# Storing the S5 inputs of a decoder trunk apart by tap instead of in token order

## The reference

```python
def s5_mix(u, ...):                                   # u: (1, 528, 256), 16 groups of 16 channels
    ...                                               # lam, bb from a, log_dt, b
    bu_re = jnp.einsum('gnc,blgc->blgn', bb_re, ug)
    bu_im = jnp.einsum('gnc,blgc->blgn', bb_im, ug)
    _, _, h_re, h_im = lax.associative_scan(complex_linear_combine, (lam_re, lam_im, bu_re, bu_im), axis=1)
    y = (jnp.einsum('gcn,blgn->blgc', c_re, h_re)
         - jnp.einsum('gcn,blgn->blgc', c_im, h_im)).reshape(bsz, length, S5_DIM)
    y = jax.nn.gelu(y + d_skip * uf)
    return y * jax.nn.sigmoid(y @ glu_w + glu_b)
```

## Time and profile before

| | us |
|---|---|
| median of three runs | 1577.77 (1576.98 to 1577.96) |
| the profiled execution | 1578.03 |
| its span, first to last instruction | 1576.3 |
| TensorE busy | 1533.4 (97%) |
| VectorE busy | 873.2 (55%) |
| ScalarE busy | 696.6 (44%) |
| passes that read UIN by tap: scan inputs, 128 | 7.8 |
| passes that read UIN by tap: kernel taps, 40 | 11.3 |

### The profile page before, as it was taken

One profiled execution on the slowest core, in us unless ns is written; L12 is line 12 of the kernel. 1 busy time (PEld: TensorE's weight loads), 2 busy tenths in 40 slices (PEclk: granted clock), 3 DMA queues, 4 the chain that ended last, 5 costly groups with the idle time before them and its releaser, 6 DMA issues.

```text
span 1576.3 us, 38948 instructions
## 1 busy us (share of the span) xinstructions
PE 1533.4 (97%) x16258; PEld 1443.3 (92%) x16258; DVE 873.2 (55%) x1487; ACT 696.6 (44%) x1120; POOL 118.4 (8%) x257
## 2 busy tenths in 40 slices
PE   8999999999999999999999999999899999999998
PEld 7899898999699999999999999965599999999886
DVE  5578744443556667666333445366556666765222
ACT  5555233333535444444222588367635444443121
POOL 1450293300000000000000000000000000000000
PEclk9999999999999999999999999999999999999999
DMA  5222000000123333233323232330023333324331
GB/s 155 68 67 81 21 4 4 4 4 4 44 68 93 93 93 87 86 93 95 99 85 86 65 92 80 84 122 1 1 81 94 93 93 93 89 86 115 94 91 72
DMA packets 210748, 113.65 MB, mean 72 GB/s; under 512 B 8032, under 2 KB 207410, under 8 KB 210642
## 3 DMA queue, kind: packets, MB, share of 16 engines
q1 hardware_dynamic: 210034, 109.93, 24.2%
q10 hardware_dynamic: 608, 2.16, 0.4%
HBM read 109.95 MB, written 2.13 MB: 71 GB/s over the span
## 4 chain that ended last, share of the span: by engine, by line
PE 90%; ACT 4%; DVE 3%; issue 2%; SPq 1%; DMA 0%; DVEq 0%; ACTq 0%
PE BK L667 88%; PE BK L1195 2%; ACT XB L1253 1%; ACT PTT L1253 1%; SPq L397 0%; ACT L1253 0%; DVE MQA L1761 0%; DVE WLO L1761 0%; ACT ALL L1253 0%; ACT WHI L1253 0%; DVE XB L1761 0%; PE BK L1129 0%; ACT PR L1253 0%; DMA PRAW<-in_ffn_conv_b_dram 0%; ACT BKV L1253 0%
## 5 line engine op out<-in xcount | busy, mean ns | idle before, releaser
L1761 DVE TENSOR_TENSOR WLO<-RAW,WHI 128x1024 fp32r<-128x1024 f32 (+1 forms) x182 | 236.2, 1298 | 135.5 <-ACT WHI L1253 134.5
L1253 ACT ACTIVATE WHI<-RAW 128x1024 fp32r<-128x1024 f32 (+1 forms) x182 | 202.7, 1114 | 222.9 <-PE BK L667 222.1
L667 PE MATMUL BK<-YNH,WLO 128*128 128x264 f32 (+1 forms) x1216 | 247.6, 285 | 0.0
L667 PE MATMUL BK<-YNH,WHI 128*128 128x264 f32 (+1 forms) x1216 | 247.4, 285 | 0.0
L667 PE MATMUL BK<-YNL,WHI 128*128 128x264 f32 (+1 forms) x1216 | 246.5, 284 | 0.0
L667 PE MATMUL BK<-XNH,WHI 128*128 128x258 f32 (+1 forms) x1056 | 216.3, 286 | 0.6 <-DVE XNL L1768 0.6
L667 PE MATMUL BK<-XNH,WLO 128*128 128x258 f32 (+1 forms) x1056 | 213.4, 284 | 0.0
L667 PE MATMUL BK<-XNL,WHI 128*128 128x258 f32 (+1 forms) x1056 | 213.0, 283 | 0.0
L667 PEld LDWEIGHTS BK<-YNH,WHI 128*128 128x128 f32 x1216 | 189.7, 189 | 0.5 <-issue 0.3
L667 PEld LDWEIGHTS BK<-YNH,WLO 128*128 128x128 f32 x1216 | 188.6, 189 | 0.0
L667 PEld LDWEIGHTS BK<-YNL,WHI 128*128 128x128 f32 x1216 | 188.1, 188 | 0.0
(11 more groups left out here) (297 smaller groups left out, 2215.3 us busy)
## 6 DMA issues: line engine op xcount, KB each, us to landing
RAW<-in_ffn_w_up_dram SPq DMA_DIRECT2D x88, 512.0 KB, 3.9
RAW<-in_ffn_w_down_dram SPq DMA_DIRECT2D x32, 704.0 KB, 4.7
RAW<-in_odd_w_in_dram SPq DMA_DIRECT2D x24, 512.0 KB, 3.9
RAW<-in_even_w_in_dram SPq DMA_DIRECT2D x22, 512.0 KB, 3.9
CB<-cum_dram SPq DMA_DIRECT2D x8, 528.0 KB, 8.2
RAW<-in_even_w_out_dram SPq DMA_DIRECT2D x8, 512.0 KB, 4.1
RAW<-in_odd_w_out_dram SPq DMA_DIRECT2D x8, 512.0 KB, 4.2
XIN<-in_x_dram ACTq DMA_DIRECT2D x4, 512.0 KB, 5.8
```

The costliest lines, as they stand in the source:

```text
L667: return pe.matmul(o, l, r, start=start, stop=stop, skip_group_check=check)
L1253: return nc.scalar.activation(o, i, f, **kw)
L1761: return nc.vector.tensor_tensor(o, x, y, op)
```

## The change

The row of UIN is laid out as (tap, block) instead of (block, tap): token 4b + l lies at 132 l + b. Four places follow from it: the view `UIN4` is now contiguous over the 132 blocks of a tap; the scaling writes its 528 elements in token order from PSUM to four places 132 floats apart; the skip connection reads and writes whole contiguous rows; and the last product reads UIN and GLS by tap and writes PT2 in token order, since the output projection wants that. GLS is in UIN's order, as it comes from matmuls over UIN's columns. No instruction is added, removed or moved.

```diff
-        UIN4 = UIN[:, :, :].rearrange("p s (b l) -> p s l b", l=S5_L)
+        UIN4 = UIN[:, :, :].rearrange("p s (l b) -> p s l b", l=S5_L)
...
                     if u >= 20:
-                        scaled("in0", UIN[:, u - 20:u - 19, :], n, slot)
+                        taps_apart = lambda ap: ap.rearrange("p a (b l) -> p a b l", l=S5_L)
+                        ve.wait_ge(S("w_used"), n + 1)
+                        tt(UIN[:, u - 20, :].rearrange("p (l a b) -> p a b l", l=S5_L, a=2),
+                           taps_apart(banks("in0", 2 * slot)), taps_apart(inverse("in0")), ALU.mult)\
+                            .then_inc(S("ps_free"), 1)
                         return
...
                     ve.wait_ge(S("s5_ymm"), t + 1)
-                    u = UIN[:, t, :].rearrange("p (b a l) -> p a l b", a=2, l=2)
+                    u = UIN[:, t, :].rearrange("p (a l b) -> p a l b", a=2, l=2)
...
                         ve.wait_ge(S("glu_sg"), t + 1)
-                        tt(PT2[:, k % 2, :], GLS[:, t, :], UIN[:, t, :], ALU.mult).then_inc(S("mx"), 1)
+                        by_tap = lambda ap: ap.rearrange("p (l b) -> p l b", l=S5_L)
+                        tt(PT2[:, k % 2, :].rearrange("p (b l) -> p l b", l=S5_L), by_tap(GLS[:, t, :]),
+                           by_tap(UIN[:, t, :]), ALU.mult).then_inc(S("mx"), 1)
```

## The result

The changed kernel takes **1572.74 us** (median of 8 runs, 1571.54 to 1574.39), against 1577.71 for the kernel before in the same comparison (8 runs, 1575.85 to 1578.07): a ratio of 0.997, 95% interval 0.9959 to 0.9981. That is faster, by 0.3%. The forecast was 1573.4. The profiled execution's span is 1571.4 us, before 1576.3.

A forecast was written before the change was run, and what follows sets the result against it. TensorE, busy 97% of the span and 90% of the chain, was taken as the bound. Terms -2.40 + 0 - 2.93 + 0.88 = -4.4 us from 1577.8 gave 1573.4 us, range 1571.5 to 1576.0.

The forecast's parts named there:

- TensorE's price of the stride: UIN passes on TensorE, scan and taps: contiguous reads take about 0.113 us per four instead of 0.238.
- rival (d): UIN passes: the 0.238 us come not from the stride but something else, TensorE stays as is; 1578.2 us, chance 0.05.
- First place: Scan inputs, 171 to 186 us: 128 passes 4.0 us shorter, VectorE becomes late, last bonus product 2.40 us earlier.
- the row of the cleared 54 elements: First place: 103 ns for 54 elements 260 bytes apart, 0.83 ns per element, used to take the UIN writes' surcharge as 0.
- The other end of the bounds: First place: upper bound for both strided UIN writes, from the skip connection's stride price, 0.88 us.
- Second place: Kernel taps, 408 to 426 us: TensorE saves 4.6 us, VectorE is next; second skip connection ends 2.93 us earlier.
- Third place: Last products of the S5 half, 436 to 443 us: two strided products cost 0.44 us each, +0.88 us.
- (a): First place: UIN writes cost what the strided skip connection does; place -1.5, sum -3.5, 1574.2 us, chance 0.18.
- (b): New TensorE gaps near 178 and 422 us: one more low-clock stretch; sum -2.8, 1575.0 us, chance 0.15.
- (c): It goes better: the present low-clock stretch vanishes or the strided products cost nothing; 1571.0 to 1572.5 us, chance 0.08.
- (e): Four changed VectorE instructions: each short run of an access pattern costs extra; slower, 1582 us at 4.5 ns, chance 0.04.

The follow-up runs named there:

- the reorder: Second skip connection moved ahead of the fifth and sixth norm outputs on VectorE: in the changed kernel 1571.84 us, in the kernel before 1577.34 us.
- e7: The changed kernel with the second skip connection moved ahead of the norms of rows 4 and 5 on VectorE: 1571.84 us, ratio 0.9961.
- the sides: The changed kernel, UIN written in runs with inputs read strided; one last product strided only on PT2's write, the other only on GLS's read: 1573.30 us.

## Why the prediction was right, and where not

**The bound and the sum.** It forecast -4.4 us; the touched stages gave -4.1, the medians -4.97 and, in the second comparison, 1577.16 to 1572.32, -4.84. The 0.8 us between are no effect that I could tie to the change. In the two profiles 0.57 lie before the scan's first pass, where both kernels do the same, and 0.37 behind the touched stages. In the timed runs the difference depends on the mean granted clock of the runs compared: at 0.999 it is 3.8 us (medians 1575.81 of 4 and 1571.98 of 7 runs), at 0.997 it is 4.8 us (1577.63 of 31 and 1572.82 of 6), at 0.998, with only two runs after, 5.2. The times alone don't fix the change's worth to better than a microsecond. So the close agreement of 1573.4 with 1572.74 is partly luck: the mechanisms by themselves gave 1577.7 - 4.1 = 1573.6.

**TensorE's price of the stride: right.** 0.113 us per four passes forecast, 0.116 measured; 4.0 us for the scan, 3.92 (7.80 to 3.88). The tap blocks, forecast at 0.11 us per pass, take (1.17 - 0.28) / 7 = 0.13, a longer first interval counted in. With it rival (d) fell: the Trainium skill's note in SBUF — State Buffer, "Door 1: The DMA port swizzle", lets fp32 be strided by 4 elements for free, and the runs show 0.238 against 0.116 us for the same passes. The same note also says that each access that crosses to a new 16-byte line pays a penalty; at a stride of 16 bytes every element is such an access, and with that sentence of it the runs agree.

**First place: the mechanism right, one term mis-sized.** Moving the bound to VectorE was forecast at -2.40, and is -2.52 with plain UIN writes. The step that failed is the one that took the UIN writes at 0, by the row of the cleared 54 elements: 0.38 us each by duration, 0.58 for both on the path. The other end of the bounds, from the skip connection, was 0.88; the skip connection, with 264 elements in an instruction, was the nearer row, and the small one, with 54, misled. I had argued that 0.83 ns per element lies under the 1.07 ns that VectorE takes anyway; the products show that it is paid on top, (1081 - 704) / 528 = 0.71 ns per element. Why the small rows show less isn't settled. With this term the first place is -1.94.

**Second place: right.** -2.93 forecast, -2.89 measured, and each part by itself: the taps alone -2.09, the skip connections' stride 0.80 (forecast 2 x 0.43). That 4.76 us saved on TensorE bring only this, because VectorE has work up to there, is shown by the reorder.

**Third place: right but for the size.** +0.88 forecast, +0.74 measured: each product lasts 0.41 us longer, not 0.44, and 0.37 of that reach the path.

**Rivals.** (a) was half right: its cause holds, at 0.58 instead of 0.88 us, so its term was nearer than the forecast's 0. Its whole sum was -3.5; the touched stages gave -4.1, the forecast said -4.4. (b) didn't come in either profile of the changed kernel, but one kernel with nearly the same gap had it (2.21 us against 1.98), and it cost 1.63 us; leaving it 0.15 and inside the range was fair. That it stayed away in the profiles was in part luck, as the gap near 49 us shows, after which the clock fell in six profiles of 13. (c) didn't come: the low stretch stayed and the products cost. (e) fell: 1081 ns for a UIN write, far under 2.0 us.

## What to carry to other kernels

Where operands can be laid out freely, put the stride on neither engine's hot reads; if some instruction has to carry it, let one carry it on all its operands at once, since the second strided operand was free here. A gain on the bounding engine is cut off by the next engine's queue: list, for the stage, when the next engine would be ready on its own, because that number (here 2.52 of 3.92 us, and 2.09 of 4.76) and not the saving is the forecast. Then look at that queue's order again: the same reorder was worth nothing before the change and 2.29 us after it.

## What the hardware showed that I had not expected

- VectorE, products of 528 fp32: 704 to 708 ns in runs, 1116 to 1125 ns with a stride of 16 bytes on one operand or on all, 1081 with only the output in four places 528 bytes apart.
- TensorE's clock after a gap isn't set by the gap's length alone. In the kernel after, 1.98 us (before 178.69) and 2.00 us (before 420.69) left it at 2.4 GHz, and 2.15 us (before 426.82) brought 1.2 GHz. But in other profiles 1.99 us (before 420.07, UIN writes plain) and 2.21 us (before 178.88, the sides) brought 1.2 GHz, and 2.15 us (before 425.64, e7) and even 2.80 us (before 421.55, skip connection strided) left it up. The same gap of 2.17 to 2.20 us near 49 us went one way in seven profiles and the other in six.
- Two executions of one kernel can differ by 1.43 us in one stretch of 250 us at full granted clock, with the distances in the stages of the change the same. At this kernel's length that and one stretch at 1.2 GHz are the size of the effects studied here, and only distances inside a stage resolved them.
